# State-space scans of a two-block network on one Trainium2 core: the four products of the rotation back go to TensorE unsummed

## The reference, cut to what matters

```
lam_bar = jnp.exp(lam * dt)                       # complex, 32 groups x 64 states
bu = jnp.einsum('bsgh,gph->bsgp', ug, b_bar)      # inputs to the states
_, states = lax.associative_scan(combine, (a_seq, bu), axis=1)   # s[t] = lam_bar * s[t-1] + bu[t]
y = jnp.real(jnp.einsum('bsgp,ghp->bsgh', states, c_mat))
y = jax.nn.gelu(y + d_skip * uf)
y = y * jax.nn.sigmoid(y @ glu_w + glu_b)
```

## Time and profile before

| what | us |
|---|---|
| median of three runs | 2334.78 |
| the profiled execution, its time | 2334.96 |
| its span (first to last instruction) | 2333.2 |
| PE busy | 2218.3 |
| DVE busy | 572.0 |
| ACT busy | 249.9 |
| POOL busy | 65.0 |
| the eight rounds of scans, from 1898.4 to 2000.85 | 102.45 |
| DVE busy in these | 96.19 |
| POOL busy in these | 49.17 |

### The profile page before, as it was taken

How to read it: one execution, slowest core, us unless ns; L and a number is a source line. 1 busy time by engine, 2 the same in 40 slices (tenths; PEclk the granted TensorE clock), 3 DMA queues, 4 the chain that set the end, 5 groups by cost and what they waited for, 6 DMA issues and landing times.

```text
span 2333.2 us, 25906 instructions
## 1 busy us (share of the span) xinstructions
PE 2218.3 (95%) x11674; PEld 1092.1 (47%) x11674; DVE 572.0 (25%) x1090; ACT 249.9 (11%) x535; POOL 65.0 (3%) x70
## 2 busy tenths in 40 slices
PE   7998899999999988997999999999999889999998
PEld 3444445788444443454333333333333254764783
DVE  1433322200024333223211000211000269442021
ACT  0123001000001230011000000000000023330000
POOL 0000000000000000000000000000000014200000
PEclk9999999999999999998999999999999989999999
DMA  8304342443353033504599999799999742216240
GB/s 329 142 23 162 123 165 108 156 167 111 109 208 140 34 141 120 197 2 198 217 396 386 387 404 377 286 388 387 387 401 397 311 164 91 108 73 252 90 162 18
DMA packets 38706, 485.31 MB, mean 208 GB/s; under 512 B 4368, under 2 KB 4400, under 8 KB 7360
## 3 DMA queue, kind: packets, MB, share of 16 engines
q1 hardware_dynamic: 35264, 465.70, 50.1%
q0 software_dynamic: 3328, 17.90, 2.0%
HBM read 482.53 MB, written 1.05 MB: 207 GB/s over the span
## 4 chain that ended last, share of the span: by engine, by line
PE 92%; DVE 4%; DMA 2%; issue 1%; ACT 1%; DVEq 0%; SPq 0%; ACTq 0%
PE pair L320 55%; PE bank L320 37%; DVE att L1260 1%; DMA norm_par<-in_norms 1%; DMA weights<-in_moe_down 1%; DMA weights<-in_w_in 0%; DVE big L1260 0%; DVE prob L1399 0%; DVE big L1499 0%; DVE att L1497 0%; DVE hT L1260 0%; ACT hT L2058 0%; DVE att L1829 0%; DVE smax L1388 0%; ACT big L2042 0%
## 5 line engine op out<-in xcount | busy, mean ns | idle before, releaser
L320 PE MATMUL pair<-weights,hT 128*128 128x512 f32 (+2 forms) x1048 | 459.0, 594 | 6.3 <-DVE hT L1260 3.4
L320 PE MATMUL bank<-weights,att 128*32 128x512 f32 x4224 | 457.8, 593 | 0.0
L320 PE MATMUL pair<-weights,big 128*32 128x512 f32 (+1 forms) x1968 | 396.0, 592 | 3.6 <-ACT big L2042 1.7
L320 PEld LDWEIGHTS pair<-weights,hT 128*128 128x128 f32 x1048 | 197.0, 192 | 244.8 <-issue 234.7
L320 PEld LDWEIGHTS bank<-weights,att 128*32 128x32 f32 x4224 | 135.0, 110 | 306.5 <-issue 306.3
L320 PEld LDWEIGHTS pair<-weights,big 128*32 128x32 f32 (+1 forms) x1968 | 153.6, 133 | 236.1 <-issue 231.5
L320 PE MATMUL pair<-hT,weights 128*128 128x256 f32 (+1 forms) x1216 | 225.8, 349 | 0.8 <-ACT hT L2058 0.8
L320 PEld LDWEIGHTS pair<-hT,weights 128*128 128x128 f32 x1216 | 203.2, 193 | 23.6 <-ACT hT L2058 1.2
L320 PE MATMUL pair<-weights,att 128*128 128x512 f32 x352 | 158.0, 606 | 10.5 <-DVE att L1497 6.0
L1618 DVE TENSOR_TENSOR big<-head_gain,bank 128x256 f32<-128x256 f32 x66 | 27.8, 422 | 424.0 <-ACT head_gain L2120 424.0
L1260 DVE COPY big<-pair 128x1024 f32<-128x1024 f32 (+2 forms) x46 | 50.0, 1086 | 276.0 <-PE pair L320 276.0
(11 more groups left out here) (235 smaller groups left out, 1242.3 us busy)
## 6 DMA issues: line engine op xcount, KB each, us to landing
weights<-in_moe_up SPq DMA_DIRECT2D x88, 2048.0 KB, 11.1
weights<-in_moe_down SPq DMA_DIRECT2D x40, 2048.0 KB, 11.7
weights<-in_w_in SPq DMA_DIRECT2D x18, 2048.0 KB, 7.7
weights<-in_ffn_up SPq DMA_DIRECT2D x11, 2048.0 KB, 7.3
weights<-in_even_in SPq DMA_DIRECT2D x10, 2048.0 KB, 8.1
weights<-in_mem_wkv SPq DMA_DIRECT2D x8, 2048.0 KB, 7.2
weights<-in_odd_in SPq DMA_DIRECT2D x8, 2048.0 KB, 7.2
norm_par<-in_norms POOLq DMA_DIRECT2D x10, 1024.0 KB, 6.3
```

Of the source, the lines that this page charges most:

```text
L320: ins = pe.matmul(o, lhsT, rhs, **flags)
```

## The change

`outputs` no longer takes two summed states but four products: C*rr and -S*ri with the real output matrix, C*ri and S*rr with the imaginary one. The sums that VectorE and GpSimd made are made by TensorE's accumulation. VectorE makes all four products itself; GpSimd keeps only the rotation of queries and keys. The wait of VectorE for GpSimd ahead of the scans goes. Two more state buffers are taken (`bias`, and the place of GpSimd's scratch in `att`), and the scratch of the rotation moves to `head_gain`.

```diff
-        pool_tmp = [att[:, a:a + 512].rearrange("p (i t) -> p i t", i=2) for a in (5120, 5632)]
+        turn_tmp = head_gain[:, 0:512]
...
-        ssm_state = [buf.rearrange("p b t n -> p (b t n)").rearrange("p (c i t) -> p c i t", c=2, i=2)
-                     for buf in (prob, probT)]
+        ssm_re = [buf.rearrange("p b t n -> p (b t n)").rearrange("p (c i t) -> p c i t", c=2, i=2)
+                  for buf in (prob, probT)]
+        ssm_im = [buf.rearrange("p (c i t) -> p c i t", c=2, i=2)
+                  for buf in (bias[:, :, :, :].rearrange("p b t n -> p (b t n)"), att[:, 5120:6144])]
...
                     pe.wait_ge(*L.next("re_ready"))
                     pe.wait_ge(*L.next("im_ready"))
-                    for part in range(2):
+                    for part, c in ((0, 0), (0, 1), (1, 0), (1, 1)):
                         for i in range(2):
                             j = 2 * b + i
                             q0, f = 32 * (j % 4), j // 4
                             ins = mm(y[q0:q0 + 32, f // 2, f % 2 * T:(f % 2 + 1) * T], ssm_c[:, part, j, :],
-                                     ssm_state[b % 2][:, part, i, :], start=(part == 0), stop=(part == 1),
-                                     skip_group_check=True)
+                                     (ssm_re, ssm_im)[part][b % 2][:, c, i, :], start=(part == 0 and c == 0),
+                                     stop=(part == 1 and c == 1), skip_group_check=True)
...
-                    if b:
-                        ve.wait_ge(*L.next("im_ready"))
...
-                    sr = ssm_state[b % 2][:, 0, :, :]
-                    tt(sr, C, rr, ALU.mult)
-                    tt(tmpA, S, ri, ALU.mult)
-                    ve.tensor_tensor(sr, sr, tmpA, ALU.subtract).then_inc(sems("re_ready"), 1)
+                    ve.tensor_tensor(ssm_re[b % 2][:, 0, :, :], C, rr, ALU.mult)
+                    ve.scalar_tensor_tensor(ssm_re[b % 2][:, 1, :, :], S, -1.0, ri, ALU.mult, ALU.mult)\
+                      .then_inc(sems("re_ready"), 1)
+                    ve.tensor_tensor(ssm_im[b % 2][:, 0, :, :], C, ri, ALU.mult)
+                    ve.tensor_tensor(ssm_im[b % 2][:, 1, :, :], S, rr, ALU.mult).then_inc(sems("im_ready"), 1)
                     ve.wait_ge(*L.next("re_ready"))
-                ve.wait_ge(*L.next("im_ready"))
+                    ve.wait_ge(*L.next("im_ready"))
...
-                for b in range(SSM_TILES // 2):
-                    S, C = sinT[:, b % 2, :, :], cosT[:, b % 2, :, :]
-                    gp.wait_ge(*L.next("scans_ready"))
-                    if b >= 2:
-                        gp.wait_ge(*L.next("states_used"))
-                    gp.tensor_tensor(ta, C, scanned[:, 1, :, :], ALU.mult)
-                    gp.tensor_tensor(tb, S, scanned[:, 0, :, :], ALU.mult).then_inc(sems("pool_step"), 1)
-                    gp.wait_ge(*L.next("pool_step"))
-                    gp.tensor_tensor(ssm_state[b % 2][:, 1, :, :], ta, tb, ALU.add).then_inc(sems("im_ready"), 1)
-                    gp.wait_ge(*L.next("im_ready"))
-                    if b in (5, 6):
-                        rotate(b - 5)
+                for t in range(NT):
+                    gp.wait_ge(*L.at("im_ready", 6 + t))
+                    rotate(t)
```

More of the change, by code:

```diff
@@ L2270, in _ @@
                 norm_params()
-                ta, tb = pool_tmp
                 def stepped(ins):
@@ L2283, in rotate @@
                     x1, x2 = qk[:, :, 0:8], qk[:, :, 8:16]
-                    t1, t2 = [ta.rearrange("p i t -> p (i t)")[:, 256 * i:256 * i + 256].rearrange("p (n w) -> p n w", w=8)
+                    t1, t2 = [turn_tmp[:, 256 * i:256 * i + 256].rearrange("p (n w) -> p n w", w=8)
                               for i in range(2)]
```

## The result

| | us |
|---|---|
| changed kernel, median of 7 runs (lowest to highest) | 2342.46 (2341.35 to 2343.14) |
| kernel before, median of 7 runs | 2333.47 (2332.24 to 2336.27) |
| ratio, with its 95% interval | 1.0035 (1.0024 to 1.0047) |
| profiled execution of the changed kernel: time, span | 2342.3, 2340.2 |
| predicted | 2341.7 (2338.0 to 2345.0) |

The change makes the kernel 0.35% slower, 8.2 us by the ratio, with an interval from 5.6 to 11; the medians themselves are 9.0 us apart. The spans of the two profiled executions differ by 7.0 us (2340.2 against 2333.2).

A forecast was written before the change was run, and what follows sets the result against it. TensorE was taken to bound the scan rounds; its added matmuls cost 8 x 0.86 = 6.9 us, the work removed from VectorE and GpSimd gained 0, so 2334.78 + 6.9 = 2341.7 us, range 2338.0 to 2345.0.

The forecast's parts named there:

- TensorE sets the pace of the rounds: Scan rounds: TensorE's period of 12.745 us, not VectorE's 12.42, bounds them; it should grow to 13.6.
- VectorE gains on it: Scan rounds: VectorE's lag behind TensorE's `inputs` falls from 1.7 us in round 2 to 0.4 in round 6.
- 0.86 us for each `outputs`, 6.9 in all: TensorE, each `outputs`: 8 more records as 4 pairs of 0.215 us, 0.86 us, over 8 rounds 6.9.
- the entering and leaving: TensorE's `outputs` block: 0.13 us, paid once per block and not again for the added matmuls.
- Nothing behind the scans gives it back: After `outputs(7)`: no later wait absorbs the delay; the trace stays as before, later by 6.9 us.
- VectorE's round falls to 10.1 us, worth nothing: VectorE in the scans: round 2.3 us shorter, from 12.42, gaining nothing because TensorE never waits for it.
- The price of 0.69 us: VectorE in the scans: duration of each product without GpSimd beside it, read from round 7.
- The last margin grows to 5.8 us: End of the scans: time between the last state being ready and `outputs(7)` starting grows from 1.2 us to 5.8.
- Rival 1: Scan rounds: VectorE sets the pace, hidden by TensorE's records; 16 us faster over 7 rounds, 2318.7 us; 2%.
- Rival 2: `outputs`: added matmuls run one after another, 1.72 us per block, 13.8 in all, 2348.6 us; 4%.
- Rivals 3 and 4: 3: cost given back behind scans or under 4.7 us, 6%; 4: new TensorE wait for products or buffer, 2349, 3%.

The follow-up runs named there:

- products_alone: Kernel before, with VectorE making both parts of the state, sums included, and GpSimd only rotating; 4 matmuls per `outputs` kept: 2335.68 us, ratio 1.0004.
- bare_changed: Changed kernel without projections inside the rounds, all behind `outputs(7)`: 2397.18 us, against 2415.9 us for the kernel before stripped likewise, its rotations behind the last round.
- four_wide_vector: Kernel before, with `outputs` once per two rounds on four tiles, four state buffers, and VectorE making both state parts: 2330.32 us, ratio 0.9979.
- tiles_in_turn: Changed kernel with the loops of `outputs` swapped, all four products of tile 0 and then of tile 1: 2349.78 us, ratio 1.0066 to the kernel before.
- four_wide_gpsimd: Kernel before, with `outputs` once per two rounds on four tiles and four state buffers, VectorE and GpSimd working as before: 2334.37 us, ratio 0.9998.

## Why the prediction was right

- **TensorE sets the pace of the rounds.** Confirmed: the period went up with TensorE's work (13.61 us, predicted 13.6), stayed when VectorE's alone fell (products_alone), and TensorE shows no wait in the scans of either. One reading was too simple: "VectorE gains on it" holds up to round 6 only. VectorE's period of 12.42 is that of rounds 2 to 5; round 6 takes 13.35 us (1972.36 to 1985.71), longer than TensorE's, since two sums of it (2.36 in place of 1.42 us) stand beside GpSimd's rotation. VectorE starts round 7 at 1985.71, 1.0 us behind the end of `inputs(7)`, and the margin of 1.2 us ahead of `outputs(7)` was enough. The two sums and the start of round 7 in the kernel before:

```profile
1975.24 2.36 DVE L1829 TENSOR_TENSOR att<-att 128x512 f32<-128x512 f32 x2
...
1985.71 2.13 DVE L1829 TENSOR_TENSOR att<-big,pair 128x512 f32<-128x512 f32 x3
```

- **0.86 us for each `outputs`, 6.9 in all.** Each block grew from 0.99 to 1.85 us, and the stretch from `inputs(1)` to the end of the scans by 6.91 us. That the entering and leaving are paid once is confirmed by the 1.85; had they been paid twice it would be 1.98.
- **Nothing behind the scans gives it back.** Confirmed: 332.3 us follow in both.
- **VectorE's round falls to 10.1 us, worth nothing.** The mechanism is confirmed, and the size is a little off: 13.61 - 3.84 = 9.77 us. The four products start 0.60 us apart, where I counted their durations of 0.69: they do not wait for one another, and the next starts while the one before finishes. Those that are linked by a semaphore start 0.72 us apart, as at 1939.20 and the next ones in products_alone. The wait of VectorE is 3.84 us a round, 3.5 predicted. The price of 0.69 us was right, but the row it came from did not show VectorE alone: GpSimd's product of round 7 started at 1993.54, 0.10 us behind VectorE's, and GpSimd's took 1.72 us. Where GpSimd was first (1917.18 against 1917.54) it took 1.57 and VectorE's 1.76. The products without GpSimd are those of the changed kernel, 0.68 to 0.69.
- **The last margin grows to 5.8 us.** It is 6.5.
- **Rival 1** (VectorE sets the pace, 2%) is refuted by products_alone; its mechanism is real where the cover is gone, as bare_changed shows, and its price of 16 us for 7 rounds was near the 18.7 measured. The 0.4 us a round that its estimate left open as possible hidden waiting is in part the change between blocks: four_wide_vector's 24 records in one block save 0.19 us.
- **Rival 2** (added matmuls one after another, 4%) did not come about: 1.85 us a block, not 2.7. Its price was right for a chain in which half of the matmuls lose their partner: tiles_in_turn, with four steps alone, four in pairs and four alone, has blocks of 2.74 us and 2349.78 us, near the rival's 2348.6.
- **Rivals 3 and 4** (given back behind the scans, a new wait of TensorE) did not come about either: 332.3 us follow, and the waits are those of before.
- **The time.** The total is 2342.46 against 2341.7. That it is met within 0.8 us is partly luck. The sum started from 2334.78, the median of three runs; the median of seven is 2333.47. The measured difference, 9.0 us by the medians and 8.2 by the ratio, is larger than the 6.9 predicted and found in the rounds; the rest is within the interval and lies ahead of the rounds or in the spread, and whether it has a cause of its own stays open.

## What to carry to other kernels

A share of busy time does not say which of two nearly full engines sets the pace; compare their periods, and look at whether the lag between them shrinks. Moving sums into TensorE's accumulation pays where VectorE is the slower engine, and costs its full matmul time where TensorE is, even if two other engines are relieved of 61 us. Matmuls with 32 columns of weights should be gathered until they fill all four groups of partitions: here the same matmuls in half as many blocks gave back 4 to 5 us, and at most 1 us, not told from none, while GpSimd still made its half of the sums.

## What the runs showed of the hardware that was not expected

- TensorE starts a matmul for another group of 32 partitions ahead of matmuls that stand before it in the program: in tiles_in_turn, while the last four records ahead of it were still to run, so that 16 records took 12 steps of 0.215 us.
- Four tiles of 32 columns run side by side as well as two in float32: 16 records in 1.00 us, where 8 took 0.99.
- Three 128x512 operations of VectorE on SBUF operands beside GpSimd cost 5.04 us, and six alone 4.1 (6 x 0.69): here GpSimd as a helper was a net loss to VectorE. The Trainium skill, in "SBUF — State Buffer", section "Who interferes with whom", says that a VectorE instruction with two SBUF inputs contends with a GpSimd instruction that reads SBUF, and calls this an exclusive lock. The 1.64 to 1.76 us beside GpSimd and 0.69 without it agree.
- A short wait of TensorE can cost nearly its own length again: in four_wide_gpsimd it waited 2.0 us, and the granted clock was 0.94 over the block of 1.07 us behind the wait and 0.90 over the next 16.46 us (part of them at 1.2 in place of 2.4 GHz), which took 1.6 us longer than at 1.00.
